# A third slot for the last piece of w_o and other orders of rings, refills and per-engine work at the stage seams of an encoder-block kernel

## The reference

```python
h = x
u = rmsnorm(h, g_mix);  z = u @ w_in        # q, k, v, latents, gates
merged = sigmoid(ga) * (oa @ w_a_out) + sigmoid(gb) * (ob @ w_b_out)
h = h + merged @ w_o
gu = rmsnorm(h, g_ffn) @ w_gate_up;  g_, u_ = split(gu)   # D_FF = 5632
h = h + (silu(g_) * u_) @ w_down
e = rmsnorm(p @ w_ple_proj, g_ple_post)     # p: 512 x 256
gate = sigmoid(rmsnorm(h, g_ple) @ w_ple_gate)
h = h + gate * e
return rmsnorm(h, g_final)
```

## Time and profile before

| | us |
|---|---|
| median of 3 runs (lowest, highest) | 2742.37 (2740.89, 2744.74) |
| the profiled execution | 2744.7 |
| its span, first to last instruction | 2742.9 |
| TensorE busy | 2692.1 (98%) |
| VectorE busy | 1895.1 (69%) |
| ScalarE busy | 1188.3 (43%) |
| GpSimd busy | 113.7 (4%) |
| mean granted TensorE clock | 0.994 |

### The profile page before, as it was taken

The page is one execution under the profiler, slowest core; times in us unless marked ns, Lnnn a source line. Parts: engine busy times, 40 slices in busy tenths (PEclk is TensorE's granted clock), DMA queues, the critical chain, the costliest instruction groups (busy, mean ns, idle before and its releaser), DMA issues.

```text
span 2742.9 us, 42144 instructions
## 1 busy us (share of the span) xinstructions
PE 2692.1 (98%) x17284; PEld 2452.8 (89%) x17284; DVE 1895.1 (69%) x2138; ACT 1188.3 (43%) x1527; POOL 113.7 (4%) x64
## 2 busy tenths in 40 slices
PE   9999999999999999999999999999989999999998
PEld 7888888888888888799999999999989999999887
DVE  6555555455665433688888888888888897888755
ACT  5334434334554233444444444444444353444543
POOL 0000000010000211100000000000000000000052
PEclk9999999999999999999999999999999999999999
DMA  6333333333323554343444444444365353433333
GB/s 217 94 94 105 106 101 100 100 92 116 95 91 109 197 199 122 115 136 112 138 139 127 132 130 136 124 131 144 112 234 166 122 191 103 166 101 101 88 97 100
DMA packets 120661, 348.33 MB, mean 127 GB/s; under 512 B 10032, under 2 KB 36784, under 8 KB 117936
## 3 DMA queue, kind: packets, MB, share of 16 engines
q1 hardware_dynamic: 113824, 333.35, 38.8%
q10 hardware_dynamic: 6672, 12.63, 1.2%
HBM read 301.90 MB, written 44.04 MB: 126 GB/s over the span
## 4 chain that ended last, share of the span: by engine, by line
PE 91%; DVE 6%; issue 1%; DMA 1%; ACT 1%; POOL 0%; SPq 0%; DVEq 0%; ACTq 0%; POOLq 0%
PE ps L573 30%; PE ps L575 30%; PE ps L574 30%; DVE arena L1917 1%; PE ps L647 1%; DVE w_lo L1910 1%; PE ps L636 0%; DVE w_lo L1535 0%; DVE lo L1910 0%; ACT w_hi L976 0%; DVE arena L1950 0%; DVE res L2071 0%; DMA arena<-hid 0%; DMA hid<-res 0%; DVE emb L2253 0%
## 5 line engine op out<-in xcount | busy, mean ns | idle before, releaser
L573 PE MATMUL ps<-arena,w_hi 128*128 128x256 f32 (+1 forms) x4174 | 1372.3, 329 | 29.6 <-DVE w_lo L1910 14.0
L575 PE MATMUL ps<-arena,w_lo 128*128 128x256 f32 (+1 forms) x4174 | 1366.6, 327 | 0.0
L574 PE MATMUL ps<-arena,w_hi 128*128 128x256 f32 (+1 forms) x4174 | 1366.3, 327 | 0.0
L573 PEld LDWEIGHTS ps<-arena,w_hi 128*128 128x128 f32 x4174 | 797.4, 191 | 104.3 <-issue 18.3
L575 PEld LDWEIGHTS ps<-arena,w_lo 128*128 128x128 f32 x4174 | 797.2, 191 | 67.3
L574 PEld LDWEIGHTS ps<-arena,w_hi 128*128 128x128 f32 x4174 | 797.5, 191 | 66.1 <-issue 0.2
L976 ACT ACTIVATE w_hi<-raw 128x1024 fp32r<-128x1024 f32 (+1 forms) x445 | 466.2, 1048 | 818.0 <-PE ps L575 796.2
L1535 DVE TENSOR_TENSOR w_lo<-raw,w_hi 128x1024 fp32r<-128x1024 f32 x216 | 276.5, 1280 | 439.6 <-ACT w_hi L976 439.2
L573 PE MATMUL ps<-arena,hi 128*128 128x256 f32 x1234 | 349.8, 283 | 6.4 <-DVE lo L1910 5.9
L574 PE MATMUL ps<-arena,hi 128*128 128x256 f32 x1234 | 349.2, 283 | 0.0
L575 PE MATMUL ps<-arena,lo 128*128 128x256 f32 x1234 | 349.2, 283 | 0.0
(11 more groups left out here) (174 smaller groups left out, 2077.9 us busy)
## 6 DMA issues: line engine op xcount, KB each, us to landing
raw<-w_gu SPq DMA_DIRECT2D x176, 512.0 KB, 4.1
raw<-w_in SPq DMA_DIRECT2D x108, 512.0 KB, 3.5
raw<-w_dn SPq DMA_DIRECT2D x64, 512.0 KB, 4.0
hid<-res SPq DMA_DIRECT2D x22, 1024.0 KB, 6.5
raw<-w_o SPq DMA_DIRECT2D x32, 512.0 KB, 3.8
raw<-w_pg SPq DMA_DIRECT2D x32, 512.0 KB, 3.7
arena<-hid SPq DMA_DIRECT2D x14, 1024.0 KB, 9.7
raw<-w_dn SPq DMA_DIRECT2D x32, 384.0 KB, 3.1
```

Source lines behind the costliest of these rows:

```text
L573: mm(out, hi, x[:, 0, :], start=start, stop=False, skip_group_check=more)
L574: mm(out, hi, x[:, 1, :], start=False, stop=False, skip_group_check=more)
L575: return mm(out, lo, x[:, 0, :], start=False, stop=stop, skip_group_check=more)
```

## The change

- **w_o.** The last piece (`N_WO + 31`) goes into the third slot `S_HI[2]`, `S_LO[2]`, which is free, so its split waits for no matmul. TensorE's last w_o group is written apart from the loop to read it there; the number of matmuls is the same. The ring of the feed-forward starts at slot 1, then 0, then 2, and the first three `hi` wait for pieces 29, 30 and 31 of w_o.
- **First unit.** In the last w_o group and unit 0, the order of ScalarE's and VectorE's steps changes: `hi(0, 1)` and `lo(0, 1)` go ahead of the last large split, `hi(0, 3)`, `lo(0, 3)`, `hi(0, 4)`, `lo(0, 4)` ahead of small ones, and `total(3, 3)` on TensorE follows product 4 instead of 3.
- **SP.** `residual_again(0)` with its wait for the 21st `hid` store moves from the top of unit 45's loads to behind `fill(1, 3)`.
- **p's split** moves from unit 61 to unit 62, and the final tiles in the units from 62..65 to 63..66.
- **E stage.** Its first three pieces take the three slots of the ring (`E_HI`), as the last unit's products 4, 5 and 6 free them, and the split of piece 1 comes ahead of the final tiles on both engines. From piece `N_E + 3` on it is `w_hi` 1, 0, 1 again, with `piece_used` as before. On VectorE the loop over i, which holds the copies of E(2i) and E(2i+1), now has ahead of them the low part of piece N_E + 3 + i, before N_E + 2 + i; on ScalarE one table load (`ln_exp_table`) moves to behind the second pair of squares.
- **Gate stage.** In group 2 the split of piece b+4 comes ahead of `after_gate(0)`, `gate_here(1)` on ScalarE and of `gate_out_tile(1)`, `emb_norm(1)` on VectorE.

```diff
+        E_HI, E_LO = ([of[i] for i in (2, 1, 0, 1)] for of in (S_HI, S_LO))
...
 
         def ring(n):
-            return 2 - n % 3
+            return (1, 0, 2)[n % 3]
...
             for v in range(UNITS):
                 last_before = {first_unit(g) + 1: g for g in (1, 2, 3)}.get(v)
-                if v == FF + 1:
-                    sp.wait_ge(hid_out, 16 * (FF // 2 - 1))
-                    residual_again(0)
                 if last_before:
...
                 if last_before:
                     fill(last_before, 3)
+                if v == FF + 1:
+                    sp.wait_ge(hid_out, 16 * (FF // 2 - 1))
+                    residual_again(0)
                 block_load(v, A21)
...
-            with pe.Fori(0, 4) as i:
+            def w_o_group(g, n, s, pieces):
+                free(g)
+                for j in pieces:
+                    pe.wait_ge(mrg_lo, 2 * j + 2)
+                    piece(n + j, j, 2 * (1 - s), [m_tile(4 * j + k) for k in range(4)], j == 0, j == 3)
+
+            with pe.Fori(0, 3) as i:
                 for s in range(2):
-                    free(i * 2 + G_WO + s)
-                    for j in range(4):
-                        pe.wait_ge(mrg_lo, 2 * j + 2)
-                        piece(i * 8 + N_WO + 4 * s + j, j, 2 * (1 - s), [m_tile(4 * j + k) for k in range(4)],
-                              j == 0, j == 3)
+                    w_o_group(i * 2 + G_WO + s, i * 8 + N_WO + 4 * s, s, range(4))
+            w_o_group(G_WO + 6, N_WO + 24, 0, range(4))
+            w_o_group(G_WO + 7, N_WO + 28, 1, range(3))
+            pe.wait_ge(w_lo_done, N_WO + 32)
+            hi, lo = as_4_by_256(S_HI[2]), as_4_by_256(S_LO[2])
+            for k in range(4):
+                for t in range(2):
+                    i = product(ps[:, t, :], hi[:, t, k], lo[:, t, k], m_tile(12 + k), False, k == 3)
+            i.then_inc(piece_used, 1)
...
-                    if v == 0 and j == 3:
+                    if v == 0 and j == 4:
...
+                if isinstance(n, int) and n == N_WO + 31:
+                    act.wait_ge(mrg_sum, 8)
+                    copy(S_HI[2], flat(raw[:, j])).then_inc(w_hi_done, 1)
+                    return
+                if isinstance(n, int) and N_E <= n < N_E + 3:
+                    act.wait_ge(s_used, 7 * LAST_UNIT + 5 + n - N_E)
+                    copy(E_HI[n - N_E], flat(raw[:, j])).then_inc(w_hi_done, 1)
                     return
...
-                if n == 0:
-                    act.wait_ge(mrg_sum, 8)
-                elif n < 3:
-                    act.wait_ge(piece_used, N_WO + 33 - n)
+                if n < 3:
+                    act.wait_ge(piece_used, N_WO + 30 + n)
...
                     x_split(B22_, SIX, res[:, 8:14, RIGHT], 0, N_WO + 30)
+                    hi(0, 1)
                     x_split(T3_, SIX, res[:, 0:6, RIGHT], 0, N_WO + 31)
-                    hi(0, 1)
...
+                    x_split(T4_, TWO, t4_last[:, :, LEFT], 15)
+                    x_split(B21_, TWO, x_last[:, :, LEFT])
+                    hi(0, 3)
+                    x_split(T2_, TWO, res[:, 6:8, LEFT], 15)
                 for k in (2 * g, 2 * g + 1):
                     square(24 + k, res[:, k, :], sq_b, emptied, G_WO + g + 1)
-            x_split(T4_, TWO, t4_last[:, :, LEFT], 15)
-            x_split(B21_, TWO, x_last[:, :, LEFT])
-            x_split(T2_, TWO, res[:, 6:8, LEFT], 15)
-            hi(0, 3)
+            hi(0, 4)
             x_split(B22_, TWO, x_last[:, :, RIGHT])
             x_split(T3_, TWO, res[:, 6:8, RIGHT], 16)
             sum_split(3)
-            hi(0, 4)
...
-                    if v == FF + 17 and j in (2, 4):
+                    if v == FF + 18 and j in (2, 4):
                         act.wait_ge(p_in, 16)
                         copy(P_T[j // 2 - 1][:, 0, :], P_IN[:, j // 2 - 1, :]).then_inc(u_hi, 1)
-                    if v in range(FF + 18, FF + 22) and j in (2, 4):
-                        final_tile(2 * (v - FF - 18) + j // 2 - 1)
-
-            ln_exp_table()
...
+            whi(N_E, 0)
             for k in range(8, 11):
                 final_tile(k)
-            act.wait_ge(s_used, 7 * LAST_UNIT + 5)
-            whi(N_E, 0)
+            whi(N_E + 1, 1)
             for k in range(11, 14):
                 final_tile(k)
-            act.wait_ge(s_used, 7 * UNITS)
-            whi(N_E + 1, 1)
+            whi(N_E + 2, 2)
             for k in range(14, 16):
                 final_tile(k)
-            for i in range(2, 6):
-                whi(N_E + i, i % 4)
-                squares(2 * i - 4, 2)
+            squares(0, 2)
+            whi(N_E + 3, 3)
+            squares(2, 2)
+            ln_exp_table()
+            whi(N_E + 4, 0)
+            squares(4, 2)
+            whi(N_E + 5, 1)
+            squares(6, 2)
...
                 if g == 2:
+                    whi(b + 4, 0)
                     after_gate(0)
...
-            lo(0, 1)
...
-            t_step(res[:, 6:8, RIGHT], x_last[:, :, RIGHT], res[:, 6:8, RIGHT])
+            lo(0, 3)
             sum_2(0)
             x_low(19, T2_, TWO, res[:, 6:8, LEFT])
-            lo(0, 3)
+            t_step(res[:, 6:8, RIGHT], x_last[:, :, RIGHT], res[:, 6:8, RIGHT])
             sum_4(0)
+            lo(0, 4)
+            sum_3(0)
             x_low(20, B22_, TWO, x_last[:, :, RIGHT])
             x_low(21, T3_, TWO, res[:, 6:8, RIGHT])
+            lo(0, 5)
             sum_low(3)
-            lo(0, 4)
-            sum_3(0)
-            lo(0, 5)
...
+            wlo(N_E, 0)
             for k in range(8, 11):
                 final_low(k)
             add_c11_c12(LAST_UNIT)
             add_u3(LAST_UNIT)
-            wlo(N_E, 0)
+            wlo(N_E + 1, 1)
             for k in range(11, 14):
                 final_low(k)
-            wlo(N_E + 1, 1)
-            final_low(14)
+            wlo(N_E + 2, 2)
+            for k in range(14, 16):
+                final_low(k)
+            add_squares(0, 2)
             for i in range(4):
-                wlo(N_E + 2 + i, (2 + i) % 4)
-                if i == 0:
-                    final_low(15)
-                add_squares(2 * i, 2)
+                if i < 3:
+                    wlo(N_E + 3 + i, (3 + i) % 4)
+                    add_squares(2 * i + 2, 2)
                 for e in (2 * i, 2 * i + 1):
...
+                if g < 7:
+                    wlo(b + 4, 0)
                 if g == 2:
                     gate_out_tile(1)
                     emb_norm(1)
-                if g < 7:
-                    wlo(b + 4, 0)
                 if g == 0:
```

More of the change, by code:

```diff
@@ L229, in flat @@
             return slot.rearrange("p t k c -> p (t k c)")
-        def as_2_by_512(slot):
-            return flat(slot).rearrange("p (k c) -> p k c", k=2)
         def sums(norm):
@@ L275, in build, with as_4_by_256 @@
         S_LO = [flat(w_lo[:, 0]), flat(w_lo[:, 1]), lo_2[:]]
+        E_HI, E_LO = ([of[i] for i in (2, 1, 0, 1)] for of in (S_HI, S_LO))
+        def as_4_by_256(slot):
+            return slot.rearrange("p (t k c) -> p t k c", t=2, k=KP)
         def columns(v):
@@ L1533, in wlo @@
                     tt(low, raw[:, j, 0, :, UPPER], low, ALU.subtract).then_inc(w_lo_done, 1)
+                    return
+                if isinstance(n, int) and n == N_WO + 31:
+                    tt(S_LO[2], flat(raw[:, j]), S_HI[2], ALU.subtract).then_inc(w_lo_done, 1)
+                    return
+                if isinstance(n, int) and N_E <= n < N_E + 3:
+                    e = n - N_E
+                    tt(E_LO[e], flat(raw[:, j]), E_HI[e], ALU.subtract).then_inc(w_lo_done, 1)
                     return
```

23 lines of the change are left out of this document (13 added, 10 removed).

## The result

The changed kernel takes 2753.94 us, median of 6 runs (2751.50 to 2756.72), against 2742.96 for the kernel before (6 runs, 2740.89 to 2745.28): a ratio of 1.0037, 95% interval 1.0025 to 1.0049, so 11 us slower. The profiled execution took 2754.02 us, its span 2752.2, against 2744.7 and 2742.9 before, so 9.3 us more. This is the side that was forecast, and 4.5 us above the point, within the range.

The account below looks back on a forecast made before the run. TensorE was taken as the bound, its small idle time lying at the seams. Terms -1.1 - 4.8 - 5.9 + 17.9 + 0.9 = +7.0 on 2744.7 gave 2751.7 us profiled, 2749.4 median; range 2741 to 2756.

Parts of the forecast that it names:

- part 4: E stage: +17.9 us; three stalls of 5.2 for late copies, 6.0 of clock, less 3.7 that goes.
- Rival 1: E stage: the copies don't bind, 17 us are gained, about 2725; chance 8%.
- Part 3: p's split, unit 61: -5.9 us; the stall of 4.1 and 1.8 of clock go.
- Part 2: Units 43 to 45, SP's order: -4.8 us, VectorE becoming the limit; ends 3 and 7 of gain.
- my signs of being wrong: VectorE not the limit in units 43 to 45, or ScalarE starting the split of N_E + 3 before E3 ends.
- the upper end: Units 43 to 45: gain of 7 if half-clock matmuls behind the 7.5 us go too and nothing else binds.
- VectorE's lead by the first fill: Units 43 to 45: VectorE 5.9 us earlier by the first fill, 5.7 by the second, less by the fourth.
- Part 1: w_o and unit 0: -1.1 us; ends -3 and +2.
- The wait of 3 to 4 us before product 4: Unit 0: sign to look for, one gap of some 3.5 us in place of 2.7 and 0.4.
- my upper end: w_o and unit 0: +2 us, if the one longer gap brings the clock down.
- I take half of the 2.2: w_o and unit 0: VectorE's low part comes 2.2 us earlier; half is taken as gain, so -1.1.
- Part 5: Gate stage: +0.9 us, a new wait of 2.6 replacing 1.74; if VectorE starts before POOL, 0.4, sum 2.2 lower.

Follow-up runs that it names:

- copies_first: Changed kernel with VectorE's two E-stage copies out of PSUM ahead of the low part of piece N_E + 3 + i and the two sums; 2731.27 us, ratio 0.9959.
- only_p: Kernel before with one edit: p's split and the final tiles one unit later; 2737.18 us, ratio 0.9982.
- only_sp: Kernel before with one edit: SP waits for the hidden stores and loads the residual behind the third fill, not ahead of the first; 2739.43 us, ratio 0.9988.
- cf_res4: copies_first with the first down unit's residual loaded behind the fourth fill, not the third; 2726.93 us.
- best: copies_first with two ScalarE snapshots of unit 0 moved earlier and the first down unit's residual behind the fourth fill; 2727.19 us, ratio 0.9945.
- copies_again: copies_first unchanged, run again on one chip with best and old_wo_res4; 2730.32 us.
- cf_old_wo: copies_first with the change to w_o's last piece, the weight ring and unit 0's order undone; 2728.41 us.
- only_gate: Kernel before with one edit: in the third gate group both parts of piece b + 4 ahead of the first gate output's steps; 2739.91 us, ratio 0.9992.
- old_wo_res4: cf_old_wo with the first down unit's residual loaded behind the fourth fill; 2726.46 us.

## Why the prediction was right, part by part

**The sign and the size** rest on part 4, and its three numbers held: stalls of 5.16 from start to start (forecast 5.2) three times, priced from the row of the kernel before in which the same instructions stood one piece later; clock losses of 2.2 each (2.0 forecast); 4.2 for what goes (3.7). Three times 0.2 more for the clock and 0.5 more for what goes cancel. Rival 1, copies that don't bind, is refuted, and copies_first shows what it would have given: 2731, not 2725. By the traces copies_first gains 14.6 up to the last norm (2731.11 to 2716.52) where rival 1 adds up 17.2: parts 1, 2 and 5 give less, part 3 and the E stage more. The rest of the 6 is for the most part the starting point, the profiled execution of before, which lies above its own median, while that of copies_first does not.

**Part 3**: cause and stall right; the 5.9 was 7.0. The mis-sized term is the clock: 1.8 forecast from the four us of the earlier trace rows, 2.9 measured (7.0 - 4.1), since the clock is half for longer than those four us: the mean of 14 us from 2412 is 0.76 in the kernel before and 1.00 in only_p.

**Part 2**: alone the step holds (4.8 forecast, 5.0 in only_sp's trace). In the changed kernel the seam gives 3.2. One of my signs of being wrong came: VectorE isn't the limit throughout. It waits 2.14 us for the fourth fill, where I had it busy without a gap. That this fill stands behind the residual's 1 MB was foreseen, but priced at 1 us less gain and not as a wait. Here the rows of the changed kernel, SP's fill 2 and residual, ScalarE's and VectorE's first instruction on fill 4:

```profile
2031.05 0.52 SPq L500 DMA_DIRECT2D arena<-hid  x1
...
2038.05 0.38 SPq L505 DMA_DIRECT2D res<-h_dram  x1
...
2055.47 1.06 ACT L986 ACTIVATE arena<-arena 128x1024 fp32r<-128x1024 f32 x1 [3.27 <-DMA arena<-hid]
...
2056.55 1.23 DVE L1943 TENSOR_TENSOR arena<-arena 128x1024 fp32r<-128x1024 f32 x1 [2.14 <-ACT arena L986]
```

The other term that I had at nothing is the clock: the 4.8 has no half clock in it, and the upper end only that behind the first wait. The seam of the changed kernel has three half-clock stretches, from 2045, 2065 and 2075, only_sp's has two, and the kernel before two (2049 to 2054 and from 2077). Up to the last wait at 2245 the changed kernel needs 2.8 more than only_sp: 1.6 for the stretch more, 0.2 in the waits of the seam (8.0 against 7.8), and the 1.0 of the second refill, which only kernels with part 1 show. The prediction's 5.9 for VectorE's lead by the first fill doesn't follow from rows 8 as it stands (2043.91 less 2037.5 is 6.4), but only_sp measured 5.9.

**Part 1** failed in sign: +1.3 for -1.1 up to the seam, and +2.3 with the second refill, for which I had no term. The wait of 3 to 4 us before product 4 came (3.31), and the clock fell behind it, which was my upper end; in the kernel before the longest wait, 2.67, left it up. Two things I had not seen. ScalarE could not begin the last piece at 1137.0, since it waited longer for the store of h, which stands ahead of it:

```profile
1137.25 0.72 ACT L986 ACTIVATE res<-res,gn 128x512 f32<-128x512 f32 x1 [2.02 <-DMA h_dram<-res]
...
1139.57 1.23 DVE L1555 TENSOR_TENSOR lo<-raw,hi 128x1024 fp32r<-128x1024 f32 x1 [3.08 <-ACT hi L986]
```

That is 1.57 behind the row (0.35 of it from further ahead; 1.04 in copies_first), and VectorE's low part, the second row, comes at 1139.57, not 1138.0. And a second snapshot, behind the root and its table load, costs 1.22 at 1176.06. The step that failed is "I take half of the 2.2": three waits, two of them for ScalarE's snapshots, 6.1 us and half clock behind the longest, replaced the four for VectorE, 5.7 us. With the two snapshots ahead the same part gains 1.1 up to the seam, the forecast's number, for a reason the forecast didn't have.

**Part 5**: the new wait is 0.71, not 2.6, so -1.0 and not +0.9. The mis-sized term is the low part's 3.41 us, which I carried over from the earlier trace rows. VectorE's low parts and GpSimd's multiplies in the changed kernel:

```profile
2626.22 2.53 DVE L1561 TENSOR_TENSOR w_lo<-raw,w_hi 128x1024 fp32r<-128x1024 f32 x1 [1.10 <-ACT w_hi L986]
...
2635.34 1.22 DVE L1561 TENSOR_TENSOR w_lo<-raw,w_hi 128x1024 fp32r<-128x1024 f32 x1
...
2625.26 2.41 POOL L2332 TENSOR_TENSOR tmp<-tmp,emb 128x1024 f32<-128x1024 f32 x1 [1.36 <-DVE emb L2218]
...
2635.43 3.38 POOL L2332 TENSOR_TENSOR tmp<-tmp,emb 128x1024 f32<-128x1024 f32 x1 [0.69 <-DVE emb L2218]
```

In the second pair VectorE started 0.09 ahead of GpSimd and took 1.22, its time alone; GpSimd's multiply took 3.38 instead of 2.41. In the first pair GpSimd was 0.96 ahead and VectorE took 2.53, to 1.08 behind GpSimd's end. 2.6 less 2.2 is 0.4, and 0.3 remain. That is the result that the prediction set beside its sum. The Trainium skill (SBUF — State Buffer, "SBUF: two separate sides") has the rule: the pair of ports goes to whichever of the two engines starts first, for the whole instruction; the trace agrees in both pairs. By it the sum would have been 2.2 lower; the error in part 5 hid part of that in parts 1 and 2.

**Of the total**, the errors are +2.4 (part 1), +1.6 (part 2), +1.0 (second refill), -1.1, 0.0 and -1.9, with 0.35 ahead of the first mark: 2.3 in the profiled execution. That the sum is this close is in part luck: the terms beside part 4 are off by 8.0 us in all, of which all but 2.0 cancel. The rest of the 4.5 is that the changed kernel's profiled execution lies at its median, while that of before lies 1.7 to 2.3 above its own, perhaps for the most part by p's wait.

## What to carry to other kernels

When an engine's list puts a buffer's release (here a copy out of PSUM) behind an instruction that waits for a later step of the same consumer, the price can be read before any run: find the row where the same order already stands elsewhere, and add up what lies ahead of the release. One such place cost 22 us and hid gains of 11, so a change of several parts is worth taking apart before it is rejected: copies_first is the change with three lines moved, and with the residual one load later (cf_res4) it is 15 us, 0.53%, under the kernel before. In these traces a stall of 2 us or more cost its length and, often but not always, 1.6 to 2.2 of half clock, and the two gains of 1 to 4 us in different seams that were tried together did not add up.

## What was not expected of the hardware

- Waits of nearly one length are followed by half clock in one execution and not in another: 1.88 (best, 2069.86) and 2.03 (copies_again, 2239.98) were, 2.67 (cf_old_wo, 1164.24) and 2.29 (copies_first, 2058.47) were not; 2.67 in only_sp was. The 2.08 ahead of the E stage was in before, only_sp and only_p, and was not in only_gate. Not even 2.97 (old_wo_res4, 2044.54) was; all of 3.0 and more in these traces were.
- VectorE's subtraction of 128x1024 took 1.22 where it started 0.09 us ahead of GpSimd's multiply, and 2.33 to 3.41 where it started behind. The one that started second paid, 1.0 us (GpSimd) or 1.1 to 2.2 (VectorE).
- A 1 MB load moved from behind the third to behind the fourth fill of one queue brought the fourth 3.2 us forward (2053.95 to 2050.76, 0.55 of which came from further ahead), while the DMA engines' mean share from 2032 to 2062 was 1.00 and 0.98.
